# Sliding attention of a two-block model: scores two units ahead, first two units inside the projection before it

## The reference, cut to what matters

```python
kw, vw = with_prev(kb), with_prev(vb)          # each block sees itself and the one before
s = einsum('bnqhgd,bnkhd->bnhgqk', qb, kw) * 64 ** -0.5
s = where(valid, s, -inf)
probs = softmax(concatenate([s, sink], -1), -1)[..., :-1]
o = einsum('bnhgqk,bnkhd->bnqhgd', probs, vw)
```

## Time and profile before

| what | value |
|---|---|
| median of 3 runs | 2001.93 us (2000.49 to 2002.12) |
| the profiled execution's own time | 2007.46 us |
| its span in the trace | 2005.6 us |
| TensorE busy | 1924.5 us, 96% |
| VectorE busy | 1370.4 us, 68% |
| ScalarE busy, GpSimd busy | 894.3 us (45%), 514.3 us (26%) |
| mean granted clock | 0.983 |
| projection `U_dz` ends, last `values` end, levels of the inverse begin | 167.03, 216.72, 258.80 us |

### The profile page before, as it was taken

One profiled execution on the slowest core, in us unless ns is written; L12 is line 12 of the kernel. 1 busy time (PEld: TensorE's weight loads), 2 busy tenths in 40 slices (PEclk: granted clock), 3 DMA queues, 4 the chain that ended last, 5 costly groups with the idle time before them and its releaser, 6 DMA issues. The chain is left out here.

```text
span 2005.6 us, 23901 instructions
## 1 busy us (share of the span) xinstructions
PE 1924.5 (96%) x8826; PEld 1562.0 (78%) x8826; DVE 1370.4 (68%) x1446; ACT 894.3 (45%) x974; POOL 514.3 (26%) x268
## 2 busy tenths in 40 slices
PE   7999999999999999999999999999999999999992
PEld 6877887888888878778887787877887787878881
DVE  5438757667677658544045563767998898989994
ACT  3224323423223442232002214136878887878873
POOL 3520014000000004625653544600322221322222
PEclk9998899999999999999999999999999999999996
DMA  5311011665562223243236262234999999999994
GB/s 175 112 63 64 24 33 57 206 201 190 191 203 97 85 88 110 79 184 104 85 105 231 84 251 63 88 137 178 370 359 372 366 368 366 376 378 372 374 338 157
DMA packets 115306, 385.37 MB, mean 192 GB/s; under 512 B 21845, under 2 KB 24196, under 8 KB 88734
## 3 DMA queue, kind: packets, MB, share of 16 engines
q1 hardware_dynamic: 98800, 349.88, 48.6%
q10 hardware_dynamic: 10382, 25.42, 3.9%
q0 software_dynamic: 6048, 9.03, 1.3%
HBM read 353.49 MB, written 43.79 MB: 198 GB/s over the span
## 5 line engine op out<-in xcount | busy, mean ns | idle before, releaser
L3054 DVE TENSOR_TENSOR m_lo<-m_raw,m_hi 128x2048 fp32r<-128x2048 f32 x200 | 448.9, 2284 | 12.0 <-ACT m_hi L2982 11.8
L2982 ACT ACTIVATE m_hi<-m_raw 128x2048 fp32r<-128x2048 f32 x200 | 383.0, 1920 | 105.3 <-DMA m_raw<-in_w_exp_gate_dram 71.4
L264 PE MATMUL ps<-xhi,whi 128*128 128x512 f32 x936 | 373.6, 399 | 7.0 <-DVE xlo L493 3.3
L266 PE MATMUL ps<-xhi,wlo 128*128 128x512 f32 x936 | 365.4, 390 | 0.0
L265 PE MATMUL ps<-xlo,whi 128*128 128x512 f32 x936 | 365.2, 390 | 0.0
L241 POOL TENSOR_SCALAR whi<-raw 128x2048 fp32r<-128x2048 f32 (+1 forms) x55 | 105.2, 1912 | 831.5 <-PE ps L266 722.1
L243 POOL TENSOR_TENSOR wlo<-raw,whi 128x2048 fp32r<-128x2048 f32 (+1 forms) x55 | 255.0, 4637 | 4.6
L264 PE MATMUL ps<-m_hi,xt_hi 128*128 128x512 f32 x544 | 216.9, 399 | 9.6 <-DVE xt_lo L3059 8.0
L264 PEld LDWEIGHTS ps<-xhi,whi 128*128 128x128 f32 x936 | 176.3, 188 | 48.6 <-issue 9.2
L265 PE MATMUL ps<-m_lo,xt_hi 128*128 128x512 f32 x544 | 213.9, 393 | 0.0
L266 PE MATMUL ps<-m_hi,xt_lo 128*128 128x512 f32 x544 | 212.8, 391 | 0.0
(11 more groups left out here) (490 smaller groups left out, 3016.9 us busy)
## 6 DMA issues: line engine op xcount, KB each, us to landing
m_raw<-in_w_exp_gate_dram SPq DMA_DIRECT2D x68, 1024.0 KB, 6.4
m_raw<-in_w_exp_up_dram SPq DMA_DIRECT2D x68, 1024.0 KB, 6.6
m_raw<-in_w_exp_down_dram SPq DMA_DIRECT2D x68, 1024.0 KB, 6.5
raw<-in_w_in_dram SPq DMA_DIRECT2D x42, 1024.0 KB, 5.2
ada_w<-in_w_ada_dram ACTq DMA_DIRECT2D x48, 512.0 KB, 4.2
y_rows<-xhi SPq DMA_DIRECT2D x39, 512.0 KB, 10.9
raw<-in_w_up_dram SPq DMA_DIRECT2D x16, 1024.0 KB, 5.6
raw<-in_w_down_dram SPq DMA_DIRECT2D x16, 1024.0 KB, 5.2
```

What stands on the lines that cost most here:

```text
L264: nc.tensor.matmul(o, lh, rh, start=start, stop=False)
L266: return nc.tensor.matmul(o, ll, rh, start=False, stop=stop)
L2982: nc.scalar.activation(m_hi[s][:], m_raw[s][:], ACT.Copy).then_inc(m_split, 1)
L3054: nc.vector.tensor_tensor(m_lo[s][:], m_raw[s][:], m_hi[s][:].bitcast(F32), ALU.subtract).then_inc(m_low, 1)
```

## The change

`scores` now run two units ahead: `scores(0)` and `scores(1)` stand inside the first chunk of the projection, the turning and the values of unit 0 inside its second chunk. In the loop the order is turning of i, `scores(i+2)`, `turn_out(i-1)`, values of i; in the last two units the place of the scores is taken by the delta steps' sums with `rows(0)`, then `rows(1)`, and `rows(2)`. VectorE no longer subtracts the maximum from the tile; it makes four columns of the negated maximum, and ScalarE takes them as the bias of the exponential, which becomes four operations of 128x256 for one of 128x1024. The columns `att_v` have three buffers for two and another place. On VectorE `shifted` runs two units ahead of `normalised`, and the differences of delta chunk 0 come ahead of `normalised(7)`. The low half of chunk `Z_CHUNK + 2` moves from behind `shifted(1)` to behind the four `items`; its high half moves on ScalarE from behind the Silu to the last unit. The programs of SyncE and GpSimd are not changed.

The tiles:

```diff
-        att_v = place("att_v", o_at + 5376, [P, 2, 32])
+        att_v = place("att_v", o_arena + 17152, [P, 3, 32])
         def score_bank(i):
-            return 2 * (i % 2) if i else 4
+            return 2 * (i % 2) if i >= 2 else 4 + 2 * i
+        step_sum = ps[:, 1, 0:TT * GH]
```

TensorE:

```diff
                     scores(0)
+                    scores(1)
+                def turns(i):
...
+                def values(i):
...
+                linear(pe, U_dz, (xhi, xlo), inside=[((0, 1), lambda: swap_key(0)), ((0, 2), lambda: swap_key(1)), ((0, 3), first_scores),
+                                                     ((4, 1), lambda: turns(0)), ((4, 2), lambda: values(0))])
...
+                scores(2)
+                for i in range(1, len(AU)):
+                    turns(i)
+                    if i + 2 < len(AU):
+                        scores(i + 2)
+                    elif i + 2 == len(AU):
+                        nc.tensor.matmul(step_sum, tri, step[:].rearrange("p t h -> p (t h)"), start=True, stop=True).then_inc(cols_pe, 1)
+                        rows(0)
+                    else:
+                        pe.wait_ge(cols_dve, 1)
+                        rows(1)
+                    turn_out(i - 1)
+                    if i + 1 == len(AU):
+                        rows(2)
+                    values(i)
+                rows(3)
+                betas(0)
                 turn_out(len(AU) - 1)
-                rows(1)
-                betas(0)
                 betas(1)
-                rows(2)
-                rows(3)
```

ScalarE:

```diff
-                    nc.scalar.activation(att_s[:, i % 2], att_s[:, i % 2], ACT.Exp).then_inc(soft_act.sem, 1)
+                    for j in range(4):
+                        ins = nc.scalar.activation(att_s[:, i % 2, j], att_s[:, i % 2, j], ACT.Exp, bias=v[:, 24 + j:25 + j])
+                    ins.then_inc(soft_act.sem, 1)
...
                     nc.scalar.activation(delta_in[:, 12 + m, :], bank(U_dz, m), ACT.Silu).then_inc(lin_free[side(U_dz)], 1)
+                    if m == 1:
+                        probs_out(0)
                 nc.scalar.preload_act_table_set(LOG_EXP)
-                act.wait_ge(split_done, Z_CHUNK + 2)
-                chunk_high(act, Z_CHUNK + 2)
+                exps(1)
...
+                for i in range(1, len(AU)):
+                    probs_out(i)
                     if i + 1 < len(AU):
                         exps(i + 1)
+                    else:
+                        act.wait_ge(split_done, Z_CHUNK + 2)
+                        chunk_high(act, Z_CHUNK + 2)
+                    high(i - 1)
```

VectorE:

```diff
-                    nc.vector.tensor_tensor(s, s, row_max.unsqueeze(2).to_broadcast([P, 4, 2 * P]), ALU.subtract).then_inc(soft.sem, 1)
+                    nc.vector.tensor_scalar(below, row_max, -1.0, None, ALU.mult).then_inc(soft.sem, 1)
...
                 shifted(0)
                 chunk_low(dve, Z_CHUNK + 1)
+                shifted(1)
...
+                for i in range(2, len(AU)):
+                    shifted(i)
+                    if i >= 3:
+                        low(i - 3)
+                    normalised(i - 2)
+                dve.wait_ge(d_c, 32)
+                dve.wait_ge(cols_pe, 1)
+                nc.vector.tensor_copy(g_col[:, 0], step_sum.rearrange("p (t h) -> p t h", h=GH)).then_inc(cols_dve, 1)
+                low(len(AU) - 3)
+                normalised(len(AU) - 2)
+                dve.wait_ge(cols_dve, 1)
+                diffs(0)
+                low(len(AU) - 2)
+                normalised(len(AU) - 1)
...
                 for c in range(TT):
                     items(c)
+                chunk_low(dve, Z_CHUNK + 2)
                 dve.wait_ge(l_in, 16 * NB)
```

More of the change, by code:

```diff
@@ L1032, in first_scores @@
                     scores(0)
-                linear(pe, U_dz, (xhi, xlo), inside=[((0, 1), lambda: swap_key(0)), ((0, 2), lambda: swap_key(1)), ((0, 3), first_scores)])
-                def turn_out(i):
-                    pe.wait_ge(*out_dve.at("norm", i))
-                    if i >= 1:
-                        pe.wait_ge(att_lo, i)
-                    for a in range(2):
-                        last = nc.tensor.transpose(att_turned(i)[:, a], att_o[:, i % 2, 2 * a:2 * a + 2, :].rearrange("p j n -> p (j n)"), ident)
-                    last.then_inc(out_turn, 1)
-                for i, (n, g) in enumerate(AU):
-                    if i + 1 < len(AU):
-                        scores(i + 1)
+                    scores(1)
+                def turns(i):
                     pe.wait_ge(*soft_act.at("exp", i))
@@ L1054, in _ @@
                             last.then_inc(turn_pe, 1)
-                    if i >= 1:
-                        turn_out(i - 1)
+                def values(i):
+                    n, g = AU[i]
                     pe.wait_ge(turn_act, 2 * i + 2)
+                    if i == 0:
+                        pe.wait_ge(*soft.at("mask", 1))
+                    else:
+                        pe.wait_ge(*out_dve.at("norm", i - 1))
                     for j in range(4):
@@ L1062, in _, with turn_out @@
                     last.then_inc(value_pe, 1)
+                linear(pe, U_dz, (xhi, xlo), inside=[((0, 1), lambda: swap_key(0)), ((0, 2), lambda: swap_key(1)), ((0, 3), first_scores),
+                                                     ((4, 1), lambda: turns(0)), ((4, 2), lambda: values(0))])
+                def turn_out(i):
+                    pe.wait_ge(*out_dve.at("norm", i))
+                    if i >= 1:
+                        pe.wait_ge(att_lo, i)
+                    for a in range(2):
+                        last = nc.tensor.transpose(att_turned(i)[:, a], att_o[:, i % 2, 2 * a:2 * a + 2, :].rearrange("p j n -> p (j n)"), ident)
+                    last.then_inc(out_turn, 1)
                 def rows(c):
@@ L1070, in betas @@
                         pe.wait_ge(kb_dve, c - 1)
-                    elif c == 1:
-                        pe.wait_ge(cols_dve, 1)
                     for h in range(GH):
@@ L1377, in exps, with probs_out @@
                 def exps(i):
-                    v = att_v[:, i % 2]
+                    v = att_v[:, i % 3]
                     act.wait_ge(*soft.at("shift", i))
-                    nc.scalar.activation(att_s[:, i % 2], att_s[:, i % 2], ACT.Exp).then_inc(soft_act.sem, 1)
+                    for j in range(4):
+                        ins = nc.scalar.activation(att_s[:, i % 2, j], att_s[:, i % 2, j], ACT.Exp, bias=v[:, 24 + j:25 + j])
+                    ins.then_inc(soft_act.sem, 1)
                     act.wait_ge(*soft.at("gap", i))
                     nc.scalar.activation(v[:, 8:12], v[:, 4:8], ACT.Exp).then_inc(soft_act.sem, 1)
[L1384 to L1388, removed]
-                act.wait_ge(split_done, Z_CHUNK + 2)
-                chunk_high(act, Z_CHUNK + 2)
[L1392 to L1396, removed]
+                def probs_out(i):
                     for half in range(2):
@@ L1402, in _, with high @@
                                              ps[:, 4 + half, :].rearrange("p (a n) -> p a n", n=P), ACT.Copy).then_inc(turn_act, 1)
-                    if i >= 1:
-                        high(i - 1)
+                exps(0)
+                for m in range(4):
+                    act.wait_ge(lin_full, 4 * U_dz + m + 1)
+                    nc.scalar.activation(delta_in[:, 12 + m, :], bank(U_dz, m), ACT.Silu).then_inc(lin_free[side(U_dz)], 1)
+                    if m == 1:
+                        probs_out(0)
+                nc.scalar.preload_act_table_set(LOG_EXP)
+                exps(1)
+                def high(i):
+                    act.wait_ge(out_turn, i + 1)
+                    nc.scalar.activation(att_slot(xhi, i), att_turned(i), ACT.Copy).then_inc(att_hi, 1)
+                for i in range(1, len(AU)):
+                    probs_out(i)
                     if i + 1 < len(AU):
                         exps(i + 1)
+                    else:
+                        act.wait_ge(split_done, Z_CHUNK + 2)
+                        chunk_high(act, Z_CHUNK + 2)
+                    high(i - 1)
                 high(len(AU) - 1)
@@ L1639, in columns @@
                 def columns(i):
-                    return (att_v[:, i % 2, 4 * q:4 * q + 4] for q in range(6))
+                    return (att_v[:, i % 3, 4 * q:4 * q + 4] for q in range(7))
                 def shifted(i):
@@ L1644, in shifted @@
                     s = att_s[:, i % 2]
-                    row_max, gap, esink, total, den, inv = columns(i)
+                    row_max, gap, esink, total, den, inv, below = columns(i)
                     dve.wait_ge(score_pe, i + 1)
@@ L1691, in low, with diffs @@
                                             ALU.subtract).then_inc(att_lo, 1)
[L1693 to L1707, removed]
-                def lower(c):
-                    dve.wait_ge(decay_act, c + 1)
-                    dve.wait_ge(kk_pe, c + 1)
```

(12 more changed lines are left out.)

10 lines of the change are left out of this document (4 added, 6 removed).

## The result

The changed kernel takes **2009.83 us** (median of 20 runs, 2001.32 to 2018.09); the kernel before took 2000.54 us beside it (20 runs, 1997.20 to 2003.50). The ratio is 1.0042, 95% interval 1.0032 to 1.0052: slower by 0.4%, about 8 to 9 us. The prediction said 2011.7 with 2001 to 2018. The profiled execution took 2001.32 us, the shortest of the 20, at a span of 1999.5 us.

A forecast was written before the change was run, and what follows sets the result against it. TensorE, busy 96%, was taken as the bound. Attention -3.7, delta rows forward -3.4, held load and stores +14.7 and clock ramp +2.2 gave +9.8 us on the 2001.93 median: 2011.7 us, range 2001 to 2018.

The forecast's parts named there:

- part 5: SyncE's queue: the moved low half holds the load and the stores behind it; +14.7 us before the small inverses.
- part 3: Attention loop two ahead: 4.3 us a unit, one half-clock stretch of some 17 us, last values end at 213.
- Part 1: Two units in the projection: it ends at 171.0, turning of unit 1 at 174.5, TensorE idles 2.4 us.
- Part 2: Shift in the exponential: VectorE's unit falls to 4.0 us; ScalarE's four exponentials take 1.5, bounds 1.14 and 1.67.
- The moment V: End of the last attention unit's values: predicted 213 us, for 216.72 before; 205.4 with the clock full throughout.
- Rival B: Clock hardly falls in the attention: last values at 205.4 to 208, total about 2004 us; chance 0.19.
- The sign by which the prediction would be wrong: For the end of the attention's last values: the prediction is wrong if it is not between 205 and 219.
- Part 4: Delta rows moved forward: last values to last `lower` takes 12.3 us, 3.4 less; the `items` of 8.0 follow.
- the two prices for load and stores: Low half to stores landed: 6.2 us if they share nothing with the load, 8.7 one after another; 8.7 taken.
- Part 6: TensorE behind the delayed inverses: some 15 us of idling, then half clock costing 2.2 us; levels begin at 268.6.
- the ramp: Dense matmuls at half clock after TensorE's long idling behind the delayed inverses: 2.2 us lost.
- The sum: All terms to the start of the inverse's levels: -3.7 - 3.4 + 14.7 + 2.2 = +9.8 us.

The follow-up runs named there:

- e1: The kernel before with only the low half of chunk 13 moved behind the four items: 2018.89 us, ratio 1.007.
- e2: The changed kernel with SyncE's load of chunk 16 put behind the read-back, so the stores are freed: 1991.08 us, ratio 0.9942 to the kernel before.
- e5: The changed kernel again, unedited: 2007.45 us, ratio 1.0028 to the kernel before.
- e7: The changed kernel with SyncE still waiting for the low half ahead of the stores, but the load behind the read-back: 2002.74 us, ratio 1.0007.
- e8: As e2, with ScalarE's exponential of unit 1 moved ahead of the four Silu: 1992.57 us, ratio 0.9953 to the kernel before.
- e9: The kernel before with e2's edit, the load of chunk 16 behind the read-back: 1999.21 us, ratio 0.9992.
- e3: As e2, with VectorE's subtraction of the maximum and the single exponential back: 1996.06 us, ratio 0.9963 to the kernel before.
- e4: As e2, with five filler matmuls behind scores(2) in TensorE's pause: 1992.28 us, ratio 0.9939 to the kernel before.
- e10: As e4, with three filler matmuls for five: 1988.89 us, ratio 0.9952 to the kernel before.

## Why the prediction held

**The mechanism and the sign are shown.** The load waited for the low half, the stores for the load, the inverses for the stores. e1 has the cost alone (14 us; part 5 had +14.7), e2 takes it away and the kernel is 11.6 us faster than before. The term for the clock in the attention, part 3, did not hold, and the number came out near in part by luck.

**Part 1.** Scores at 171.17 for 171.0, the turning of unit 1 at 174.94 for 174.5, the pause 2.64 for 2.4: right.

**Part 2.** Four exponentials: 1.70 us for the 1.5 taken, outside the bounds of 1.14 to 1.67. The upper bound, made of the 1.14 us for 128 columns and the added columns at the whole tile's rate, was 0.03 too low, and I chose below it without a row that asked for it. The pause came out 0.2 us longer for it.

```profile
173.19 1.70 ACT L1397 ACTIVATE att_s<-att_s,att_v 128x256 f32<-128x256 f32 x4
```

The Trainium skill (ScalarE: Activation LUTs, What ACT_TABLE_LOAD costs) gave 1.7 us by estimate, and the trace agrees: 1.70.

**Part 3.** A unit of 4.3 us measured 4.05 to 4.25. The moment V is the mis-sized term: 213 predicted, with 17 us at the half clock; measured 204.7 with none (the trace after), 205.2 (e5) with a short stretch, 209.2 (e2) with some 10 us. One stretch of 17 us was taken, and no trace of the changed kernel has it. Rival B, with a chance of 0.19, had V at 205.4 to 208, and by the trace after and e5 it is what happened in the attention. The sign by which the prediction would be wrong, V before 205, came true by 0.3 us in the first of them. B's time, about 2004, is not what the median says, however.

**Part 4.** V to the last `lower` 12.37 us for 12.3, the `items` 8.0 for 8.0.

**Part 5.** From V to the end of the low half 22.65 for 22.5. Low half to read-back 9.0 for 8.7, read-back to inverses 5.1 for 5.25, VectorE idle 14.10 for about 14. Of the two prices for load and stores the upper was right, though its 3 us for the four stores came from no row; the lower, 6.2 without the load's share, measures 4.8 in e7. The Trainium skill (DMA: Bandwidth & Descriptors, Queues, rings and completion order) has the descriptors of a ring taken in order; e7's 4.2 us less without the load agrees, but transfers that shared the engines' time would give the same, and no run tells these apart.

**Part 6.** Idling 16.6 for about 15, the ramp 1.7 for 2.2. That the ramp comes from the long idling is not borne out: e2 idles 2.56 us there and loses 1.6, while in e8, whose clock stayed full after 2.58 us, the levels begin 17.04 us behind the small inverses, within 0.2 of before.

**The sum** of +9.8 us stands beside 9.3 in the medians of the first runs and 8.2 in e5's. With the terms as measured against the trace it was worked out on, it is -12.0 - 3.4 + 14.9 + 1.7 = +1.2 us, which is, to rounding, the +1.3 of the levels: they start at 260.06 for a forecast of 268.6. So the sum is 8.5 us too high where it was worked out, by the 8.3 us of V, and the agreement with the medians is in part luck.

What is shown of the gap between traces and medians is this. Against e9's trace, from an execution of the more frequent kind, the change costs 4.8 to 5.9 us by the start of the levels. From there to the first expert matmul eleven of the 13 traces take 1113.8 to 1114.2 us (e3 and e1 take 1.5 and 2.4 more), so what is won or lost by the levels is still there. The stage behind it, from the first expert matmul to the first fetch of the results, is untouched by every edit and takes 590.1 to 603.5 us in the 13 traces, so a single execution's time is uncertain by more than the effect. It was 593.7 in the first profiled execution of the changed kernel and 600.9 in e5's, which is 7 of the 8 us between their times.

What is argued only: over the 20 runs of the changed kernel the time falls by some 1.6 us for each 0.001 of mean granted clock (correlation -0.79), and their mean is 0.9826 where the profiled one had 0.985. So the median execution may have about 4 us more time by its clock than the profiled one, which would fit a half-clock stretch in the attention in many of them, as taken in part 3; where it lies was not seen. The fillers (e4, e10) kept the clock full in the attention of their traces and showed no gain in the median, which speaks against it, if weakly. With e9's trace as the measure, 2 to 5 us of the 8 to 9 remain open.

## What to carry to other kernels

An instruction that is moved carries its semaphore with it. List who waits for that semaphore, and what stands behind each of those waits in the waiter's own program: here a split of 2.3 us, which cost nothing on its own engine, held back the stores in another engine's queue, and VectorE stood idle for 14 us. Where a prefetch in a queue waits for a late event, put it behind the transfers that are urgent: that edit of two lines takes the changed kernel from 0.4% slower to 0.6% faster than the kernel before, and no version measured is clearly better (e4, e8 and e10 can't be told from it).

## What was not expected of the hardware

After the same pause of TensorE, 2.64 us with the same TensorE program, the granted clock stayed full in two executions (the changed kernel's first trace and e7), was half for some 3 us in another (e5: 0.91, then 0.66) and for some 10 us in a fourth (e2, below), so that a single trace does not tell what a pause costs.

```profile
172.00:176.00 4.00, 1.36 (x10) 0.96 (x7) 3.18 (x9) 3.19 (x7) 0.00 (x0) 0.82 0.00 0
...
180.00:184.00 4.00, 4.00 (x21) 4.00 (x21) 3.18 (x9) 0.22 (x2) 0.00 (x0) 0.50 0.00 0
```

A filler matmul whose operands are both f32, 128x512, shows as two records and takes some 0.9 us at the full clock (4.56 for five, 2.84 for three), where the split matmuls of that width start 0.23 us apart. The spread of the changed kernel's first runs, 2001 to 2018, is far wider than that of the kernel before beside it, 1997 to 2003.5. It is not a property of the change: beside e5 to e8 the kernel before went from 1991 to 2013.
